# A transformer kernel in float32r: the two rings of split weight tiles are moved by 80 and by 208 bytes in SBUF

## The chip, the core and the metric

The kernel runs on one core of one Trainium2 chip. The metric is the device time of the program in microseconds. Three runs of the kernel before gave 2170.07, 2169.03 and 2170.19 us, median 2170.07 us.

## The reference

The input is a sequence of 256 tokens with 2048 features, batch 1. Everything is float32. The work is a chain of projections with small mixers between them:

```
h = rmsnorm(x);  proj = h @ w_in                      # 2048 x 7184
x = x + [stick_breaking(...), gated_delta(...)] @ w_out
x = x + cross_attention(rmsnorm(x), mem) @ w_xo
x = x + conv_ffn(rmsnorm(x)) : @ w_up (2048 x 11264), conv, silu, @ w_down
h = rmsnorm(x);  p = h @ fox_w_in                     # 2048 x 8224
x = x + (fox_attention(...) * silu(gate)) @ fox_w_out
h = rmsnorm(x);  p = h @ swa_w_in                     # 2048 x 4608
x = x + (window_attention(...) * silu(gate)) @ swa_w_out
return rmsnorm(x)
```

The weights come to about 370 MB and each is used once.

## The kernel before, in words

**The arithmetic.** Each float32 operand of a projection is split into two float32r tiles whose sum is close to it: hi (the value rounded to float32r) and lo (the rest). A product is taken as hi x hi + hi x lo + lo x hi, three passes in place of a slower full-float32 matmul.

**The weight stream.** SyncE loads the weights in order into `RAW`, a ring of `NRAW` = 5 tiles of 1024 floats in each of the 128 partitions. Each tile has two halves of 512 floats; there are 1416 halves in all (`HALVES`). For each half j ScalarE copies `RAW` to `WH[:, j % 6, :]` as float32r (the tile WH, line 1655, is the helper that records it), and VectorE subtracts `WL = RAW - WH` (line 987). The rings `WH` and `WL` hold `NW` = 6 halves each, 2048 bytes per partition and half. ScalarE works up to 5 halves ahead of TensorE (`HI_AHEAD`) and VectorE up to 4 (`LO_AHEAD`). SyncE refills a `RAW` tile when VectorE is done with it.

**The main matmuls.** `main(j)` of the TensorE program waits for `s_lo` to reach j + 1, that is for WL of half j, and then issues the matmuls of the half through the helper `mm` (line 510). A matmul has a stationary operand (loaded by LDWEIGHTS, 128 columns) and a moving operand. In the profile "main<-A,WH" means the output `main`, the moving tile A and the stationary tile WH. The activations lie in `A`, `B`, `H` and `M`; for each of their 128-row blocks 256 floats of hi and 256 floats of lo stand side by side, 2048 bytes in all. There are three forms of a half:

- wide (1184 halves, and 8 of the key and value projection of the window attention): 8 matmuls. WH is stationary and hi and lo of the activation move together (512 columns), twice; WL is stationary and hi moves (256 columns), twice; and all of this for two blocks, so 4 matmuls of 512 columns and 4 of 256.
- tokens (176 halves): 6 matmuls of 512 columns. The activation is stationary and WH, WL, WH move.
- plain or small (40 halves, and 8 more of the key and value projection, whose token part moves 256 columns): 12 matmuls of 256 columns.

That is 1192 x 8 + 176 x 6 + 48 x 12 = 9536 + 1056 + 576 = 11,168 main matmuls. The mixers and norms run between them in the same queues, in an order fixed when the program is built (`interleave`, with the tables `T_...`); their outputs are called `two`.

**Addresses.** The helper `at(name, kb, ...)` puts a tile at a base plus kb KB in every partition. All operands of main matmuls start at the base plus a multiple of 512 bytes: `A` at 16 KB, `B` and `H` at 48 KB, `M` at 80 KB, `RAW` at 163 KB, `WH` at 183 KB, `WL` at 195 KB, and within the tiles every slice starts at a multiple of 512 bytes. `WH` and `WL` are written by ScalarE and VectorE alone, and read by VectorE (WH) and TensorE (both). No DMA touches them.

Of the kernel before, what the change touches and what calls it, by code (L numbers as in the profile page):

```python
# [9 lines left out]
R = mybir.dt.float32r  # L10
# [5 lines left out]
NRAW, NW, HI_AHEAD, LO_AHEAD = 5, 6, 5, 4  # L16
# [249 lines left out]
def program(nc, xT, memT, ws, par, cst, g2, cscr, out):  # L266
    with ExitStack() as ctx:
# [44 lines left out]
        def at(name, kb, shape, dt=F):  # L312
            return nc.alloc_sbuf_tensor_at(name, [128] + shape, dt, offset=off0 + int(kb * 1024))
# [8 lines left out]
        RB, RB2 = at("RB", 160, [T]), at("RB2", 161, [T])  # L322
        SM = at("SM", 162, [256])
        RAW = at("RAW", 163, [NRAW, 1024])
        WH, WL = at("WH", 163 + 4 * NRAW, [NW, 512], R), at("WL", 163 + 4 * NRAW + 2 * NW, [NW, 512], R)

        M, MS = at("M", 80, [16, 2, T], R), at("MS", 112, [16, T])
        MH, ML = M[:, :, 0, :], M[:, :, 1, :]
# [1887 lines left out]
```

How the kernel before makes its waits and increments, by code:

```python
    def wait_ge(self, sem, value):  # L163
        if self.seen.get(sem.name, 0) < value:
            self.seen[sem.name] = value
            self.engine.wait_ge(sem, value)
# [288 lines left out]
        def sync_program(e):  # L455
# [2 lines left out]
            def load(i):  # L458
                if i >= NRAW:
                    w.wait_ge(s_lo, 2 * (i - NRAW) + 2)
                e.dma_start(RAW[:, i % NRAW, :], ws[i]).then_inc(s_raw[i % NRAW], 16)
# [15 lines left out]
            def swap(r):  # L477
                src, dst = wide_to(*ROPED[r]), ROT[r % 2]
                w.wait_ge(s_scl, SCALED[ROPED[r]])
                w.wait_ge(rp_zero, 1)
                if r >= 2:
                    w.wait_ge(rp_done, r - 1)
                for base in (0, 64):
                    lower, upper = slice(base, base + 8), slice(base + 8, base + 16)
                    e.dma_start(dst[lower, :, :], src[upper, :, :]).then_inc(s_rot[r % 2], 16)
                    e.dma_start(dst[upper, :, :], src[lower, :, :]).then_inc(s_rot[r % 2], 16)
# [6 lines left out]
                    e.dma_start(PAR[:, n:P_END], par[:, n:P_END]).then_inc(s_par2, 16)  # L494
                    e.dma_start(CST[:], cst).then_inc(s_cst, 16)
            for t, n, ve, ac in ((0, 0, 1, 0), (0, 3, 1, 1), (0, 1, 2, 1), (0, 2, 3, 1), (1, 0, 4, 1), (1, 1, 4, 2), (1, 3, 5, 2)):
                w.wait_ge(fin_ve, ve)
                w.wait_ge(fin_ac, ac)
                cols = slice(512 * n, 512 * n + 512)
                e.dma_start(out[128 * t:128 * t + 128, cols], YT[:, t, cols]).then_inc(s_out, 16)
            e.wait_ge(s_out, 128)
```

## Time and profile before

| | kernel before |
|---|---|
| device time, median of 3 | 2170.07 us |
| span of the profiled execution, first to last instruction | 2167.6 us |
| TensorE matmul (PE) busy | 2156.3 us, 99% |
| TensorE weight loads (PEld) busy | 1865.8 us, 86% |
| VectorE (DVE) busy | 1618.3 us, 75% |
| ScalarE (ACT) busy | 1327.2 us, 61% |
| GpSimd (POOL) busy | 9.7 us |
| moved by DMA | 389.31 MB, mean 180 GB/s |
| granted TensorE clock, mean | 0.999 |

How to read it: busy time counts from the start to the recorded end of each instruction. Matmuls overlap in the pipeline, so a matmul of 512 columns is recorded with some 395 ns although the next one starts after some 230 ns. What a stream of matmuls costs is therefore read from the distance between starts, not from the mean duration. The profile page gives no time of the profiled execution outside its span; the span lies 2.5 us below the median of the timed runs.

### The profile page before, as it was taken

How to read it: one execution, taken by the hardware profiler on the slowest of the kernel's cores; microseconds unless marked ns; L12 is line 12 of the kernel's file. 1: busy time of each engine (PE TensorE's matmuls, PEld its weight loads, DVE VectorE, ACT ScalarE, POOL GpSimd, SP SyncE). 2: the span in 40 equal slices, each digit the busy share in tenths (PEclk: the TensorE clock that was granted, in tenths of full speed). 3: DMA queues.
4: the chain of work that ended last, by engine and by line, in shares of the span. 5: the costliest groups of instructions: out<-in, count | busy, mean ns of one | idle time of the engine just before them, and what ended most of it. 6: DMA issues, size and time to landing. Idle time of an engine off the chain costs nothing.

```text
span 2167.6 us, 34503 instructions
## 1 busy us (share of the span) xinstructions
PE 2156.3 (99%) x13406; PEld 1865.8 (86%) x13406; DVE 1618.3 (75%) x2945; ACT 1327.2 (61%) x2601; POOL 9.7 (0%) x22
## 2 busy tenths in 40 slices
PE   9999999999999999999999999999999999999998
PEld 8888888888888888888888888888888888888887
DVE  7898666786688877655778867777676767688774
ACT  7866447775576666544666656555556655567764
POOL 0000000000000000000000000000000000000000
PEclk9999999999999999999999999999999999999999
DMA  7443434665455555555555555545554455544453
GB/s 279 169 146 137 147 115 141 218 217 186 156 190 189 188 191 186 193 185 192 187 191 189 185 194 185 193 171 197 181 177 174 167 192 186 189 161 155 146 200 140
DMA packets 107619, 389.31 MB, mean 180 GB/s; under 512 B 12304, under 2 KB 12560, under 8 KB 106688
## 3 DMA queue, kind: packets, MB, share of 16 engines
q1 hardware_dynamic: 105264, 377.31, 50.2%
q0 software_dynamic: 1904, 9.47, 1.2%
q8 instruction: 106, 1.74, 0.3%
q14 instruction: 57, 0.47, 0.1%
q10 hardware_dynamic: 288, 0.32, 0.0%
HBM read 384.34 MB, written 2.13 MB: 178 GB/s over the span
## 4 chain that ended last, share of the span: by engine, by line
PE 95%; DVE 3%; ACT 1%; issue 0%; DMA 0%; SPq 0%; DVEq 0%; ACTq 0%
PE main L510 88%; PE two L510 6%; PE two L513 1%; DVE WL L987 1%; DVE gt L987 0%; DMA RAW<-ws 0%; DVE GQ L993 0%; ACT L1654 0%; ACT WH L1655 0%; DVE GK L993 0%; PE main L556 0%; ACT PP L1655 0%; DVE PB L987 0%; ACT NT L1655 0%; DVE PP L993 0%
## 5 line engine op out<-in xcount | busy, mean ns | idle before, releaser
L1655 ACT ACTIVATE WH<-RAW 128x512 fp32r<-128x512 f32 x1416 | 882.1, 629 | 657.6 <-PE main L510 651.1
L987 DVE TENSOR_TENSOR WL<-RAW,WH 128x512 fp32r<-128x512 f32 x1416 | 961.2, 687 | 383.9 <-ACT WH L1655 374.4
L510 PE MATMUL main<-A,WH 128*128 128x512 f32 (+1 forms) x3680 | 1141.9, 393 | 1.0 <-DVE WL L987 1.0
L510 PEld LDWEIGHTS main<-A,WL 128*128 128x128 f32 x3584 | 673.9, 188 | 154.8
L510 PE MATMUL main<-A,WL 128*128 128x256 f32 x3584 | 713.7, 278 | 0.0
L510 PEld LDWEIGHTS main<-A,WH 128*128 128x128 f32 x3680 | 562.7, 189 | 13.8 <-issue 9.3
L510 PE MATMUL main<-H,WH 128*128 128x512 f32 x704 | 221.1, 395 | 0.0
L510 PE MATMUL main<-B,WH 128*128 128x512 f32 (+1 forms) x640 | 184.4, 373 | 0.0
L510 PEld LDWEIGHTS main<-H,WL 128*128 128x128 f32 x704 | 132.3, 188 | 31.3
L510 PE MATMUL main<-H,WL 128*128 128x256 f32 x704 | 138.4, 278 | 0.0
L510 PE MATMUL main<-WH,A 128*128 128x512 f32 (+1 forms) x448 | 137.6, 380 | 0.0
L510 PEld LDWEIGHTS main<-B,WL 128*128 128x128 f32 x576 | 108.5, 188 | 22.7
L510 PE MATMUL main<-B,WL 128*128 128x256 f32 x576 | 118.8, 279 | 0.0
L510 PEld LDWEIGHTS main<-H,WH 128*128 128x128 f32 x704 | 107.2, 189 | 0.0
L510 PEld LDWEIGHTS main<-B,WH 128*128 128x128 f32 x640 | 98.1, 189 | 0.2
L510 PEld LDWEIGHTS main<-WH,A 128*128 128x128 f32 x448 | 82.3, 188 | 15.4 <-DVE WL L987 0.5
L993 DVE SCALAR_TENSOR_TENSOR CC<-UB,PAR,CC 128x256 f32<-128x256 f32 x176 | 84.7, 481 | 3.1
L510 PE MATMUL main<-WL,A 128*128 128x512 f32 (+1 forms) x224 | 84.0, 375 | 0.0
L510 PE MATMUL main<-WH,B 128*128 128x512 f32 x256 | 80.2, 391 | 0.0
L510 PEld LDWEIGHTS main<-WH,B 128*128 128x128 f32 x256 | 48.1, 188 | 10.0 <-issue 0.2
L987 DVE TENSOR_TENSOR XT<-XT,main 128x512 f32<-128x512 f32 x72 | 49.1, 686 | 4.4 <-PE main L510 3.3
L1655 ACT ACTIVATE CC<-UB,PAR 128x256 f32<-128x256 f32 x88 | 51.7, 588 | 0.0
(322 smaller groups left out, 1722.5 us busy)
## 6 DMA issues: line engine op xcount, KB each, us to landing
RAW<-ws SPq DMA_DIRECT2D x707, 512.0 KB, 3.3
CB<-cscr POOLq DMA_DIRECT2D x4, 1024.0 KB, 4.7
XT<-xT POOLq DMA_DIRECT2D x4, 512.0 KB, 6.0
MS<-memT POOLq DMA_DIRECT2D x4, 512.0 KB, 8.7
xs<-xT SPq DMA_DIRECT2D x7, 256.0 KB, 7.6
out<-YT SPq DMA_DIRECT2D x7, 256.0 KB, 2.6
CST<-cst SPq DMA_DIRECT2D x1, 1248.0 KB, 7.9
G<-g POOLq DMA_DIRECT2D x1, 1024.0 KB, 5.9
```

What stands on the lines that cost most here:

```text
L510: return e.matmul(o, l, r, start=start, stop=True, skip_group_check=True)
L513: return e.transpose(o, i, ident)
L987: return e.tensor_tensor(o, a, b, op)
L993: return e.scalar_tensor_tensor(o, a, s, b, op0, op1)
L1655: return e.activation(o, i, f, bias=bias, scale=scale, accum_out=accum)
```

## The change

```
-        WH, WL = at("WH", 163 + 4 * NRAW, [NW, 512], R), at("WL", 163 + 4 * NRAW + 2 * NW, [NW, 512], R)
+        WHS, WLS = at("WH", 163 + 4 * NRAW, [512 * NW + 24], R), at("WL", 163 + 4 * NRAW + 2 * NW + 0.125, [512 * NW + 24], R)
+        WH, WL = (x[:, 20:20 + 512 * NW].rearrange("p (a b) -> p a b", b=512) for x in (WHS, WLS))
```

The two rings are allocated 24 floats (96 bytes) longer. The view of each begins 20 floats (80 bytes) into its allocation, and the allocation of WL begins 128 bytes later than before. So every half of WH lies 80 bytes further on than it did, and every half of WL 80 + 128 = 208 bytes further on. The halves are still 2048 bytes apart. `RAW` and the activations stay. No instruction is added, removed or moved on any engine, and no wait changes; only the start addresses of the operands WH and WL differ.

## Rows read from the trace of the kernel before

**Rows 1.** The page: span, busy time and the granted clock in 40 slices.
```profile
span 2167.6 us, 34503 instructions
PE 2156.3 (99%) x13406; PEld 1865.8 (86%) x13406; DVE 1618.3 (75%) x2945; ACT 1327.2 (61%) x2601; POOL 9.7 (0%) x22
...
PEclk9999999999999999999999999999999999999999
```

**Rows 2.** The page: chain of work that ended last, by engine and line.
```profile
PE 95%; DVE 3%; ACT 1%; issue 0%; DMA 0%; SPq 0%; DVEq 0%; ACTq 0%
```

**Rows 3.** Waits of PE: engine, line, waited for, total us, times, longest.
```profile
PE main L510 <- DVE WL L987: 1.0, 2, 0.5
```

**Rows 4.** Timeline of PE, a wide stretch: start, length, instruction, count.
```profile
1000.68 0.62 PE L510 MATMUL main<-H,WH 128*128 128x512 f32 x2
1001.14 0.40 PE L510 MATMUL main<-H,WL 128*128 128x256 f32 x2
1001.37 0.63 PE L510 MATMUL main<-H,WH 128*128 128x512 f32 x2
...
1004.16 0.63 PE L510 MATMUL main<-H,WH 128*128 128x512 f32 x2
```

**Rows 5.** Timeline of PE, a token stretch.
```profile
1406.66 0.39 PE L510 MATMUL main<-WL,A 128*128 128x512 f32 x1
1406.89 0.62 PE L510 MATMUL main<-WH,A 128*128 128x512 f32 x2
...
1411.42 0.39 PE L510 MATMUL main<-WL,A 128*128 128x512 f32 x1
```

**Rows 6.** Timeline of PE, two plain stretches.
```profile
25.45 0.40 PE L510 MATMUL main<-A,WH 128*128 128x256 f32 x2
25.69 0.28 PE L510 MATMUL main<-A,WL 128*128 128x256 f32 x1
...
28.33 0.40 PE L510 MATMUL main<-A,WH 128*128 128x256 f32 x2
...
581.86 0.40 PE L510 MATMUL main<-B,WH 128*128 128x256 f32 x2
...
583.66 0.40 PE L510 MATMUL main<-B,WH 128*128 128x256 f32 x2
```

**Rows 7.** Windows: stretch, us, busy per engine (count), clock, DMA share, GB/s.
```profile
26.00:28.00 2.00, 2.00 (x19) 2.00 (x19) 2.00 (x3) 1.87 (x4) 0.00 (x0) 1.00 0.98 404
582.00:584.00 2.00, 2.00 (x19) 2.00 (x18) 1.88 (x4) 1.00 (x2) 0.00 (x0) 1.00 0.00 0
```

**Rows 8.** Timeline of PE, float32 matmuls of the cross attention in a row.
```profile
577.82 3.18 PE L510 MATMUL two<-XPT,memV 128*128 128x256 f32 x14
```

**Rows 9.** The tile memV on PE: min/median/max ns, first and last start.
```profile
L510 PE MATMUL two<-XPT,memV x16: 377/379/380, 577.8 to 581.0; 128*128 128x256 f32 x16
```

**Rows 10.** Timeline of PE, float32r matmuls of the stick-breaking attention.
```profile
330.94 0.22 PE L510 MATMUL two<-SBH,NEGO 128*128 128x128 f32 x1
331.00 0.27 PE L510 MATMUL two<-SBL,NEGO 128*128 128x128 f32 x1
```

**Rows 11.** Timeline of PE, a token stretch just after an interruption.
```profile
1394.14 0.40 PE L510 MATMUL main<-WL,A 128*128 128x512 f32 x1
1394.37 0.62 PE L510 MATMUL main<-WH,A 128*128 128x512 f32 x2
...
1395.52 0.39 PE L510 MATMUL main<-WL,A 128*128 128x512 f32 x1
```

**Rows 12.** The page, part 5: busy us, mean ns of one, idle before, releaser.
```profile
L1655 ACT ACTIVATE WH<-RAW 128x512 fp32r<-128x512 f32 x1416 | 882.1, 629 | 657.6 <-PE main L510 651.1
L987 DVE TENSOR_TENSOR WL<-RAW,WH 128x512 fp32r<-128x512 f32 x1416 | 961.2, 687 | 383.9 <-ACT WH L1655 374.4
```

## The prediction

> **What bounds the kernel now.** I read the page's busy shares first. TensorE is busy for 2156.3 of 2167.6 us at the full granted clock in all 40 slices [rows 1]. The chain of waits then shows that 95% of what set the end is TensorE [rows 2]. The list of waits shows that TensorE waited for WL, the tile that each half needs last, for 1.0 us in the whole program [rows 3]. So the kernel lasts as long as the stream of matmuls lasts, and the question is what one main matmul costs from its start to the start of the next, because the change touches nothing but the addresses of one operand of each.
>
> The timelines give that distance. In the token form 21 matmuls lie between the starts at 1406.66 and 1411.42 us, so 4.76 / 21 = 226.7 ns for 512 columns [rows 5]. In the plain form 24 lie between 25.45 and 28.33, so 120.0 ns for 256 columns [rows 6]. The difference, 106.7 ns for 256 more columns, is 0.4167 ns a column, one column per cycle at the 2.4 GHz that the clock row grants. What is left is the same in both: 226.7 - 213.3 = 120.0 - 106.7 = 13.3 ns for each matmul that no column accounts for. In the wide form 20 matmuls lie between 1000.68 and 1004.16 [rows 4], five groups of two of 512 and two of 256 columns, 696 ns a group; longer stretches of the same pattern give 696.7. The columns take 640, so 56.7 / 4 = 14.2 ns are left for each matmul. Over the program that is 9536 x 14.2 + 1632 x 13.3 = 135.4 + 21.7 = 157 us, 7% of the span. This is the only thing that a shift of WH and WL could touch on the path.
>
> **The change part by part.** It adds no instruction, no wait and no DMA. Three kinds of access get a new start address.
>
> (a) ScalarE writes WH: 1416 times 629 ns. It idles 657.6 us before these, nearly all of it for TensorE to free a slot [rows 12]. (b) VectorE reads WH and writes WL: 1416 times 687 ns, with 383.9 us idle before them [rows 12]. I take both at zero. Their cover is that idle time, and the lead of 4 to 5 halves, about 1.39 us each, that the rings allow. Were (b) slower by a tenth, 1416 x 69 ns = 97 us more work would stand against those 383.9 us of idle time, and VectorE would be busy 79% instead of 75%. TensorE would see only what falls into the stretches where VectorE is full, such as 26 to 28 us [rows 7], at most a few us. A faster (a) or (b) is worth no more than the 1.0 us of rows 3. If TensorE gets faster, the cover shrinks: at 5% less time VectorE would be at 79% too, which still holds.
>
> (c) TensorE reads WH and WL, as stationary operand in the wide and plain forms and as moving operand in the token form. The trace of before has no main matmul whose operands start at anything but multiples of 512 bytes from one base, so the price of another start isn't in it, and I bound it from rows.
>
> What are the 13.3 to 14.2 ns? They are not other engines or DMA in the way. The plain form takes 120.0 ns between 26 and 28 us with DMA at 404 GB/s and ScalarE 94% busy, and again 1.80 us / 15 = 120.0 ns at 582 us with no DMA at all and ScalarE at half [rows 6, 7]. Nor are they what every weight change costs: the float32 matmuls on memV come 14 in 3.18 us, the last one counted with its whole 379 ns, so (3.18 - 0.38) / 13 = 215.4 ns each [rows 8, 9]. They have the same 128-column load and the same 512-byte starts, and if they stream their 256 columns twice (two records stand for each call), 213.3 ns are columns and 2.1 are left. And it isn't one constant: a float32r matmul of 128 columns was followed after 60 ns, 6.7 above its 53.3 [rows 10]. So the loss goes with float32r operands read at full rate while a load reads beside them. That can lie in the reading, which addresses might move, or in how the array takes in float32r weights, which they can't.
>
> *Fewer.* At the far end all but 2.1 ns goes: 9536 x 12.1 + 1632 x 11.2 = 133.7 us, giving 2036 us. With the 6.7 ns of rows 10: 9536 x 7.5 + 1632 x 6.6 = 82.3 us, giving 2088. With only the wide form brought down to the 13.3 of the other forms: 9536 x 0.9 = 8.6 us, giving 2161.5. *More.* Just after an interruption token matmuls came 6 in 1.38 us, 230 ns each, 3.3 above their steady 226.7 [rows 11]: the same operands, only the two streams of reads in another phase to each other. Paid always, that is 11,168 x 3.3 = 36.9 us, giving 2207.
>
> I take zero. The row nearest to "another relation of addresses" is the steady loss itself. It is 13.3 ns whether weights are stationary or moving, for slots of WH 2 KB apart and for slices that start 0, 512, 1024 and 1536 bytes into them. A read that depended on where its partner stands would be expected to show some spread over these, and 24 plain matmuls in a row show none. The sum is then 2167.6 + 0 for the span, which with the 2.5 us between span and median is 2170.1 us.
>
> The Trainium skill ("SBUF — State Buffer", section "Who interferes with whom") says that TensorE has two independent read ports, one for the moving operand and one for weight loads, and that it never waits on anyone. By that rule the change is worth nothing. The trace agrees that no other engine delays it, but it does show 13.3 ns a matmul that two independent ports would leave unexplained, where the same skill ("TensorE: Matmul & The Clock Gate", "Back-to-back issue gap") gives about 2.5 ns; so I don't let the rule decide.
>
> **The rivals.**
>
> *Faster: the loss is a collision of two reads at equal phase.* Both operands start at the same place within 512 bytes and both begin to be read at about the same moment, so load and stream may hit the same part of the memory again and again. With the weights 80 or 208 bytes further on they would pass each other. For it: the 2.1 ns left where the moving operand is read at half the rate, and the phase dependence in rows 11. Against it: the loss doesn't change with any step the trace holds, and two streams that stall each other once are out of phase from then on, whatever their addresses. Its price lies between the 8.6 us and the 82.3 us above; I name the middle, 45 us, 2125 us. That all of it goes (2036) is a small part of this case.
>
> *Slower: a read that begins off a boundary touches one piece more.* If TensorE fetches 64 bytes or more at once, a load of 512 bytes that starts 80 bytes in needs one more fetch, and so does each moving read of 1 or 2 KB in the token form. The place is each main matmul, where no slack covers it: the 0.2% that decides is 4.3 us / 11,168 = 0.39 ns, one cycle. With pieces of 128 bytes a load takes 5 instead of 4; if the loss goes with the pieces, a quarter of 13.3 is 3.3 ns, which is also the price of rows 11. The time lies between 2174 and 2207, and I name 2190. Against it: nothing in the trace speaks of such pieces.
>
> The Trainium skill ("SBUF — State Buffer", "The DMA port swizzle (why [64,N] ≈ [32,N])") gives the lines of SBUF 16 bytes. 80 and 208 are 5 and 13 of these, so by this rule no access touches a line more and this rival falls away. No row here shows the size of a line.
>
> *The change doesn't do what it says*, because the base is itself no multiple of 512: then only the distance between operands matters, and that does change, by 80 and 208. This gives no time of its own.
>
> **How the numbers follow.** A measurement of this kernel tells a change from none at about 0.2%, 4.3 us. No change, 2170: 0.45, with its own range of 2166 to 2174. Faster by the collision: 0.34, of which 0.07 lies below 2100. Slower by more pieces: 0.21, of which a good half lies below 2190. The effect has only to reach one cycle a matmul to leave the middle case, so I don't give that more. The range goes from 2100 to 2190 and leaves out 0.07 below and some 0.09 above.
>
> **What would show it.** If I am right, the starts in the same three stretches lie 226.7, 120.0 and 174.2 ns (the wide mean) apart again, and ScalarE and VectorE keep 629 and 687 ns. The collision is shown by shorter distances at the same clock, and best by a plain or token stretch below 13 ns of rest. The pieces are shown by longer ones in all forms. A change in 629 or 687 ns with TensorE unchanged would show that (a) or (b) is touched and covered. I am wrong if the distances move by as much as half a nanosecond, or if PE begins to wait for WL.

## The result and the profile after

The changed kernel takes 2179.38 us (median of 4, 2178.98 to 2179.54) where the kernel before takes 2169.8: a ratio of 1.0044, 95% interval 1.0032 to 1.0056. It is slower by 9.6 us. No change had been forecast, with 0.45; slower had 0.21.

The page of the changed kernel, its span, busy times and clock, answers to [rows 1]:

```profile
span 2177.7 us, 34503 instructions
...
PE 2165.4 (99%) x13406; PEld 1869.8 (86%) x13406; DVE 1619.7 (74%) x2945; ACT 1327.4 (61%) x2601; POOL 9.7 (0%) x22
...
PEclk9999999999999999999999999999999999999999
```

Its groups of the two ring operations answer to [rows 12]:

```profile
L1656 ACT ACTIVATE WH<-RAW 128x512 fp32r<-128x512 f32 x1416 | 882.5, 629 | 667.4 <-PE main L511 660.2
L988 DVE TENSOR_TENSOR WL<-RAW,WH 128x512 fp32r<-128x512 f32 x1416 | 962.2, 688 | 391.5 <-ACT WH L1656 381.1
```

ScalarE and VectorE take what they took, 629 and 688 ns; they only idle 10 and 8 us longer, which is the longer span. The clock is the same. What is new is the distance between the starts of matmuls. The timeline of PE in a wide stretch, against [rows 4]:

```profile
1005.29 0.62 PE L511 MATMUL main<-H,WH 128*128 128x512 f32 x2
1005.75 0.40 PE L511 MATMUL main<-H,WL 128*128 128x256 f32 x2
...
1009.49 0.62 PE L511 MATMUL main<-H,WH 128*128 128x512 f32 x2
```

Six groups of four in 4.20 us, 700.0 ns a group for 696.7, so 175.0 ns a matmul for 174.2. In a token stretch, against [rows 5]:

```profile
1416.71 0.40 PE L511 MATMUL main<-WL,A 128*128 128x512 f32 x1
...
1420.91 0.40 PE L511 MATMUL main<-WL,A 128*128 128x512 f32 x1
```

18 matmuls in 4.20 us, 233.3 ns for 226.7. Of the undisturbed token halves 73 take 1380 ns, which is 230.0 ns a matmul, and 27 take 1400, which is 233.3. And in two plain stretches, against [rows 6]:

```profile
25.24 0.40 PE L511 MATMUL main<-A,WH 128*128 128x256 f32 x2
...
28.42 0.40 PE L511 MATMUL main<-A,WH 128*128 128x256 f32 x2
...
586.07 0.40 PE L511 MATMUL main<-B,WH 128*128 128x256 f32 x2
...
589.67 0.40 PE L511 MATMUL main<-B,WH 128*128 128x256 f32 x2
```

27 matmuls in 3.18 us, 117.8 ns for 120.0, so faster; and 30 in 3.60 us, 120.0 as before. One change of address makes the wide and the token form dearer and one plain stretch cheaper.

Since both programs issue the same matmuls in the same order, the 13,405 distances can be subtracted one by one. The differences by form add up to the whole change of the span:

| distances | us |
|---|---|
| after wide matmuls | +6.78 |
| after token matmuls of 512 columns | +3.27 |
| after plain matmuls, and token ones of 256 columns | -1.04 |
| three long gaps at the program's start | +1.06 |
| everything else | +0.05 |
| sum | +10.12 (the spans: 2177.7 - 2167.6) |

The three gaps lie within the first 12 us. The waits for WL there rose from 1.0 to 2.1 us in all. In the other kernels below the same gaps grew by 0.05 to 1.7 us, by 0.5 us in the control e4, in which no steady distance changes, so they aren't put down to this change.

### The profile page after: what moved, and what is told of

Same layout as the page of the kernel before. It is cut to its first block, busy times and chain, and to the rows that moved or that the text cites. A ratio compares the mean times of both kernels' runs of the same rounds, so it can differ in the third digit from the quotient of the medians.

```text
span 2177.7 us, 34503 instructions
## 1 busy us (share of the span) xinstructions
PE 2165.4 (99%) x13406; PEld 1869.8 (86%) x13406; DVE 1619.7 (74%) x2945; ACT 1327.4 (61%) x2601; POOL 9.7 (0%) x22
## 4 chain that ended last, share of the span: by engine, by line
PE 95%; DVE 3%; ACT 1%; issue 0%; DMA 0%; SPq 0%; DVEq 0%; ACTq 0%
PE main L511 88%; PE two L511 6%; PE two L514 1%; DVE WL L988 1%; DVE gt L988 0%; DMA RAW<-ws 0%; DVE GQ L994 0%; ACT L1655 0%; ACT WH L1656 0%; DVE GK L994 0%; PE main L557 0%; ACT PP L1656 0%; DVE PB L988 0%; ACT NT L1656 0%; DVE PP L994 0%
```

## The experiments

Three theories went in. **D, distance**: the cost of a matmul depends on the distance between the start of the stationary and of the moving operand. **P, pieces**: each operand that starts off a boundary costs extra by itself. **N**: no address matters, only the history of the stream. Later ones are L and A (is it the weight load's reads, or the array) and M (several rhythms). The code is shortened: 183 and 195 stand for the sums of the kernel's line, and the `rearrange` of the change is left out.

### e1: a map of the shifts

```
for d in range(0, 128, 4): SECTIONS.append(("wide", d, 0, 48))     # stationary shifted by 4 d bytes
for d in range(0, 128, 4): SECTIONS.append(("plain", d, 0, 32))
for d in range(0, 128, 4): SECTIONS.append(("tokens", 0, d, 36))   # moving operand (the weights) shifted
...                                                                # wide, both or the moving operand shifted; shifts of 4 to 20 bytes
```

> A kernel of its own that computes nothing of the reference: streams of float32r matmuls on 128 rows and 128 stationary columns, in sections, with a pause between sections. Sections have the wide, plain and token forms of the kernel, with the stationary or the moving operand shifted by 0 to 496 bytes in steps of 16, a few with both shifted, and a few with shifts of 4 to 20 bytes. Theory D (distance): the two reads of TensorE meet in the memory, so the cost of a matmul varies up and down with the distance between the two starts, and both shifted by the same amount cost what no shift costs: wide 174.2 ns a matmul, plain 120.0, tokens 226.7 at distance 0, and some other distances cost less. Theory P (pieces): an operand that starts off a boundary costs more whatever the other does; then all shifts off the boundary cost the same, some 0.8 ns more in the wide form and 3 to 7 ns more in the token form, both shifted cost more still, and no shift costs less than 0. Theory N (no addresses): the times follow from the history of the stream alone; then every section of a form costs the same.

In the timeline of PE each section of one shape is one row: start, length, count. Two rows of the plain form (0 and 64 bytes), then four of the token form (0, 64, 240 and 256 bytes):

```profile
305.52 4.09 PE L82 MATMUL main<-A,W 128*128 128x256 f32 x32 [0.26 <-DVE T L69]
...
322.92 3.90 PE L82 MATMUL main<-A,W 128*128 128x256 f32 x32 [0.26 <-DVE T L69]
...
444.47 8.45 PE L82 MATMUL main<-W,A 128*128 128x512 f32 x36 [0.26 <-DVE T L69]
...
480.01 8.52 PE L82 MATMUL main<-W,A 128*128 128x512 f32 x36 [0.26 <-DVE T L69]
...
578.10 8.79 PE L82 MATMUL main<-W,A 128*128 128x512 f32 x36 [0.26 <-DVE T L69]
587.17 8.45 PE L82 MATMUL main<-W,A 128*128 128x512 f32 x36 [0.26 <-DVE T L69]
```

The lengths hold the first matmuls of each section too, so the steady distances of its last matmuls are used from here on, in ns:

| shift, bytes | 0 | 16 | 64 | 80 | 128 | 192 | 208 | 240 | 256 |
|---|---|---|---|---|---|---|---|---|---|
| wide, stationary shifted | 174.2 | 176.7 | 173.4 | 176.1 | 174.2 | 172.5 | 175.3 | 175.8 | 174.1 |
| plain, stationary shifted | 120.0 | 118.3 | 113.3 | 118.5 | 118.4 | 117.8 | 116.7 | 120.0 | 120.0 |
| tokens, moving shifted | 226.7 | 231.7 | 228.9 | 231.1 | 232.9 | 233.3 | 230.0 | 236.7 | 226.7 |

At shift 0 the bare streams give to a tenth what the kernel gives, so the loss belongs to TensorE alone. It goes up and down with the shift, and the token form repeats after 256 bytes at each of its 16 steps, to 0.1 ns. The two other forms repeat from 0 to 256 bytes, but not at each step: the wide form takes 176.7 ns at 160 bytes and 175.0 at 416, the plain form 113.3 at 64 and 117.8 at 320. Each section was started once here, and e12 shows that one start needn't speak for all. Both operands shifted alike by 32, 64, 128 or 256 bytes give 174.1 to 174.2, as none does; by 16 bytes 173.3 and by 80 bytes 175.0. N falls. P falls, since some shifts are cheaper. D holds in part: the relation of the two starts counts, but a common shift of 16 or 80 bytes isn't quite neutral, so the distance alone isn't all. That the two reads meet in the memory, as D has it, is not shown by this.

### e2, e3, e4: one ring at a time, and a control

```
e2:  WHS = at("WH", 183 + 64 / 1024, [512 * NW + 8], R);  WH = WHS[:, 4:4 + 512 * NW]     # 80 bytes;  WL: + 512 bytes
e3:  WH as before;  WLS = at("WL", 195 + 192 / 1024, [512 * NW + 8], R);  WL = WLS[:, 4:4 + 512 * NW]   # 208 bytes
e4:  WH and WL both + 512 bytes
```

> WH alone is shifted by 80 bytes; WL lies 512 bytes further on, which keeps it on a multiple of 512. Results of the changed kernel: wide halves 1400.0 ns for 1393.3, token halves 1380 to 1400 for 1360, plain halves on A 1413.6 for 1440. Theory D: half of the pairs of reads change their distance, WL keeps the old one; the wide half lands between or elsewhere (1385 to 1400), the time at 2165 to 2180 us. Theory P: half of the loads and all hi reads pay: wide 1396.7, about 2175 us. Theory N: 2169.8 or 2179.4 us, by the history only.

> WL alone is shifted by 208 bytes; WH stays. Theory D: again another mix of distances, 2165 to 2180 us, and with the kernel that shifts WH alone it need not add up to the 9.6 us of the change. Theory P: the other half of the loads pays, wide 1396.7 ns a half, about 2174 us, and the two single shifts add up to the 9.6 us. Theory N: 2169.8 or 2179.4 us.

> Both rings are shifted by 512 bytes, a control. Theory D and theory P, if the length that counts divides 512: nothing changes, halves at 1393.3, 1360 and 1440 ns, 2169.8 us within 0.1%. If a longer period than 512 bytes counts, or if any move of the rings changes the time, it differs by 0.2% or more.

| | us | ratio, 95% interval | wide half, ns | token half, ns |
|---|---|---|---|---|
| e2, WH + 80 | 2170.49 | 1.0003 (0.9993 to 1.0012) | 1387 to 1389, 1396 to 1397 | 1383 to 1391 |
| e3, WL + 208 | 2172.91 | 1.0014 (1.0005 to 1.0023) | 1393, some 1400 | 1387 |
| e4, both + 512 | 2169.85 | 0.9999 (0.9989 to 1.0008) | 1393 | 1360 |

The two single shifts cost 0.5 and 3.0 us against the same runs of the kernel before, together 3.5, where the change costs 9.6. The interval of e2 holds 1, so its time alone says little; its halves say more, since most are shorter than 1393 ns, where P had 1396.7. So the two don't add up, as P had them do, and what counts is a pattern over the reads of both rings. The control changes nothing: to move both rings by 512 bytes is free.

### e5: every pair of shifts

```
SECTIONS = [("wide", a, b, 40) for a in range(0, 256, 16) for b in range(0, 256, 16)]     # WH + a, WL + b
SECTIONS += [("tokens", a, b, 24) for a in range(0, 256, 16) for b in range(0, 256, 16)]
...
SECTIONS += [(f"w{w}", a, 0, 32) for w in (128, 256, 384, 512) for a in (0, 64, 80, 192)]     # w moving columns
```

> A kernel of its own that computes nothing of the reference: the streams of the first map again, now with two rings as in the kernel, every pair of shifts of WH and WL from 0 to 240 bytes in steps of 16, in the wide and the token form, and four widths of the moving operand. Theory D (distance, read by read): each load meets the moving read that runs beside it, so the cost of a wide group depends on both shifts and is not the sum of the two single ones; the pair (80, 208) shows the 175.0 ns a matmul that the changed kernel shows, (80, 0) and (0, 208) show less, as the two kernels with one ring shifted do. Equal shifts repeat the first map: 64 gives 173.4 and 192 gives 172.5 ns. Theory P (pieces) has fallen already if shifts of 64 and 192 are again below 174.2. The part above the columns should be about 7 ns for 128 moving columns and 13 from 256 on, if it belongs to the load that runs beside, and grow with the width if it belongs to the moving read alone.

| WH, WL | 0, 0 | 80, 208 | 80, 0 | 0, 208 | 64, 64 | 192, 192 | 128, 240 | 240, 192 | 64, 0 |
|---|---|---|---|---|---|---|---|---|---|
| wide, ns | 174.1 | 175.0 | 173.8 | 174.2 | 173.4 | 172.5 | 171.6 | 171.7 | 178.3 |
| tokens, ns | 226.7 | 230.0 | 230.9 | 230.9 | 228.8 | 233.3 | 231.2 | 233.3 | 233.3 |

The pair of the change shows its 175.0. Priced with 9536 wide and 1056 token matmuls, some 205 of the 256 pairs would be slower than no shift by more than 4.3 us, some 40 within that and some ten faster. In the token form no pair is below the 226.7 of equal starts. For an arbitrary shift, slower was the likely result. Each pair was started once, and the two that the map made the fastest, (128, 240) and (240, 192), are slower than no shift in the kernel (e9, e10).

The widths went against what [rows 10] had suggested. A stream of 128 moving columns comes every 111.7 ns, 58 above its columns, at all four shifts tried; 256 columns lose 6.7 to 13.3 and 512 columns 13.4 to 20.0 with the shift. The single 60 ns of [rows 10] was one distance between others, and no steady cost.

### e6 and e7: equal shifts of 64 and of 192 bytes

```
WHS = at("WH", 183 + 192 / 1024, [512 * NW], R);  WLS = at("WL", 195 + 192 / 1024, [512 * NW], R)     # e7; e6 with 64
```

> Both rings shifted by 64 bytes. Theory D with the numbers of the first map: wide 173.4 for 174.2 ns, 9536 x 0.8 = 7.6 us less; tokens 228.9 for 226.7, 1056 x 2.2 = 2.3 us more; plain up to 6.7 less on 576, at most 3.8 us less. Sum: 5.3 to 9.1 us faster, 2161 to 2165 us. Theory P: slower, 2174 us or more. Theory N: as before.

> Both rings shifted by 192 bytes. Theory D with the numbers of the first map: wide 172.5 for 174.2 ns, 9536 x 1.7 = 16.2 us less; tokens 233.3 for 226.7, 1056 x 6.7 = 7.0 us more; plain 2.3 less on 576, 1.3 us less. Sum: 10.5 us faster, 2159.5 us. Theory P: slower, 2174 us or more. Theory N: as before.

e6 takes 2162.72 us, ratio 0.9966 (0.9954 to 0.9979); e7 takes 2160.94 us, ratio 0.9958 (0.9945 to 0.9972). Both were forecast from the map, 2161 to 2165 and 2159.5. Both are faster than both kernels of this case. The timeline of e7 in a wide stretch:

```profile
899.94 0.62 PE L513 MATMUL main<-H,WH 128*128 128x512 f32 x2
...
903.39 0.62 PE L513 MATMUL main<-H,WH 128*128 128x512 f32 x2
```

20 matmuls in 3.45 us, 172.5 ns; its token halves take 1400 ns for 1360.

### e8: which operand, which type

```
SECTIONS = [("r", w, c, s, 32) for w in (512, 256) for c in (32, 64, 96, 128) for s in (0, 64, 80, 128, 192, 240)]   # float32r, c stationary columns
SECTIONS += [("f", w, 128, s, 24) ...]   # float32
SECTIONS += [("b", w, 128, s, 32) ...]   # bfloat16
SECTIONS += [("r", 512, 128, s, 32) for s in range(0, 64, 4)]
```

> A kernel of its own that computes nothing of the reference: streams of matmuls with 512 and 256 moving columns, with 32, 64, 96 and 128 stationary columns and six shifts of the stationary operand, in float32r; the same with 128 stationary columns in float32 and bfloat16; and shifts of 0 to 60 bytes in steps of 4. Theory L (the reads of the load that runs beside hold up the moving read): the part above the columns falls with the number of stationary columns, 13.4 ns with 128, some 6.7 with 64 and 3.4 with 32 at shift 0, and depends on the shift; bfloat16, whose operands are half as many bytes, loses less than half and float32 next to nothing. Theory A (the array takes in float32r weights slowly): the part is the same 13.4 ns with 32 as with 128 stationary columns, or follows the columns without any dependence on the shift.

The timeline of PE, whole sections: float32r with 32 stationary columns (shifts 64 and 80), with 128 (0 and 64), float32 with 256 columns (0 and 64), and bfloat16 (128 and 240; in the first of these two one record is missing):

```profile
33.07 7.60 PE L70 MATMUL main<-A,WH 128*32 128x512 f32 x32 [0.26 <-DVE T L59]
40.96 7.52 PE L70 MATMUL main<-A,WH 128*32 128x512 f32 x32 [0.26 <-DVE T L59]
...
167.26 7.57 PE L70 MATMUL main<-A,WH 128*128 128x512 f32 x32 [0.26 <-DVE T L59]
175.12 7.74 PE L70 MATMUL main<-A,WH 128*128 128x512 f32 x32 [0.26 <-DVE T L59]
...
443.82 10.63 PE L70 MATMUL main<-AF,WF 128*128 128x256 f32 x48 [0.26 <-DVE T L59]
454.73 10.63 PE L70 MATMUL main<-AF,WF 128*128 128x256 f32 x48 [0.26 <-DVE T L59]
...
566.92 7.08 PE L70 MATMUL main<-AB,WB 128*128 128x512 bf16 x31 [0.26 <-DVE T L59]
...
581.66 7.08 PE L70 MATMUL main<-AB,WB 128*128 128x512 bf16 x32 [0.26 <-DVE T L59]
```

Steady distances above the columns, for 512 moving columns in float32r: 13.3 to 20.0 with 128 stationary columns, 13.3 to 20.0 with 96, 15.0 to 22.2 with 64 and 15.6 to 18.3 with 32. A quarter of the load costs no less here. With 256 moving columns a smaller load costs somewhat less: the mean loss over the six shifts is 11.6 ns with 128 stationary columns, 10.6 with 96, 9.6 with 64 and 8.1 with 32, where L had a quarter. So L falls in its main point: the loss isn't in proportion to what the load reads, though at 256 columns it falls with it. A falls as well: the loss depends on the shift at every number of columns. bfloat16 takes 215.8 ns at all six shifts, 2.5 above its columns, and float32 takes 215.8 for 256 columns and 429.2 for 512, at all six shifts too. With 256 and 512 columns and over these six shifts, float32r is the only one of the three types that has the loss and feels the address. Even 4 bytes count: float32r with 512 columns takes 226.7 at 0 and 232.3 at 4 bytes.

### e9, e10, e11: the best and the worst pairs of the map in the kernel

```
e9:   WH + 128, WL + 240      e10:  WH + 240, WL + 448      e11:  WH + 64, WL + 512     (bytes)
```

> WH shifted by 128 bytes and WL by 240, the best pair of the map of pairs. Theory L with the map: wide 171.6 for 174.1 ns a matmul, 9536 x 2.5 = 23.8 us less; tokens 231.2 for 226.7, 1056 x 4.5 = 4.7 us more; sum 19 us faster, 2151 us. If the map's single value was a chance of how the section began, the time is anywhere from 2155 to 2175 us.

> WH shifted by 240 bytes and WL by 448, which is 192 in a period of 256: the second best pair of the map. Wide 171.7 for 174.1 ns, 22.9 us less; tokens 233.3, 7.0 us more; sum 16 us faster, 2154 us.

> WH shifted by 64 bytes, WL by 512, so by 0 in the period: the worst pair of the map. Wide 178.3 for 174.1 ns, 40 us more; tokens 233.3, 7 us more; sum 47 us slower, 2217 us. Theory P, which counts each start by itself, would put it between the kernel before and the one with both rings shifted by 64, 2163 to 2170 us.

e11 came nearly as priced: 2210.45 us for 2217, ratio 1.0183 (1.0169 to 1.0197), wide halves 1427 ns. But e9 takes 2176.7 us, ratio 1.0028 (1.0018 to 1.0039), and e10 2176.84, ratio 1.0031 (1.002 to 1.0043): slower by some 6 us where 19 and 16 less were expected, and e9 also lies outside the 2155 to 2175 us that its expectation kept for the case of chance. The timeline of e9 shows why, in two wide stretches:

```profile
899.63 0.63 PE L513 MATMUL main<-H,WH 128*128 128x512 f32 x2
...
903.14 0.64 PE L513 MATMUL main<-H,WH 128*128 128x512 f32 x2
...
1760.20 0.61 PE L513 MATMUL main<-B,WH 128*128 128x512 f32 x2
...
1763.63 0.61 PE L513 MATMUL main<-B,WH 128*128 128x512 f32 x2
```

3.51 us for 20 matmuls, 175.5 to rounding (halves of 1407 ns, 175.9), and 3.43 us, 171.5 (halves of 1373). The relative addresses are the same in both. Of its undisturbed wide halves 725 take 1406 or 1407 ns and 267 take 1373 or 1374. The stretches are long: 526 halves in a row from 626 us on take 1406 or 1407, 92 in a row from 1723 us on 1373 or 1374. No two halves that follow each other undisturbed lie on different levels; between a stretch of one and a stretch of the other there is always an interruption by a mixer. e10 has both levels too, 1400 ns in 785 halves and 1373 or 1374 in 133.

### e12: the same pairs, started at different moments

```
+ e.matmul(main[:, 1, 0:first], WH[:, 0:128], A[:, 0:first], ...)      # first = 32, 56, ... 296 columns, ahead of each section
PAIRS = [(0, 0), (80, 208), (80, 0), (192, 192), (128, 240), (240, 192), (64, 0)]
```

> A kernel of its own that computes nothing of the reference: the wide form with seven pairs of shifts, each started twelve times behind one float32r matmul of another width (32 to 296 columns), 56 matmuls each; and the token form with three pairs. Theory M (several steady rhythms): the addresses decide which rhythms exist, the moment at which a stream starts decides which of them it falls into. Then the pair (128, 240) shows 171.6 ns a matmul in some of its twelve sections and 175.9 in others, as the kernel with this pair did in its stretches (halves of 1373 and 1407 ns), (240, 192) shows 171.6 and 175.0, and the pair (0, 0) and (192, 192), whose kernels showed one level each (1393 and 1380 ns), keep to 174.2 and 172.5 nearly always. The pair (80, 208) of the change shows 175.0. Theory D alone (addresses decide everything): one level for each pair, the same in all twelve sections, and what the kernels showed of two levels came from their other instructions.

The timeline of PE in two sections with the pair (128, 240), the first started behind 32 columns, the second behind 152:

```profile
522.96 0.63 PE L76 MATMUL main<-A,WH 128*128 128x512 f32 x2
...
528.59 0.63 PE L76 MATMUL main<-A,WH 128*128 128x512 f32 x2
...
575.29 0.61 PE L76 MATMUL main<-A,WH 128*128 128x512 f32 x2
...
580.78 0.61 PE L76 MATMUL main<-A,WH 128*128 128x512 f32 x2
```

32 matmuls in 5.63 us, 175.9 ns, and in 5.49 us, 171.6. Steady distances over the twelve starts:

| wide, WH, WL | ns, in how many of twelve sections |
|---|---|
| 0, 0 | 174.2 in 12 |
| 80, 208 | 175.0 in 12 |
| 80, 0 | 173.9 in 12 |
| 192, 192 | 172.5 in 12 |
| 128, 240 | 175.8 in 7, 171.7 in 5 |
| 240, 192 | 175.0 in 7, 171.7 in 5 |
| 64, 0 | 178.3 in 12 |

The token form has 226.7 in 12 with (0, 0), 233.3 in 12 with (192, 192), and 230.0 in 10 and 233.3 in 2 with (80, 208); the changed kernel has both of these, in halves of 1380 and 1400 ns. M holds for the pairs tried: the addresses decide which steady rhythms exist, and the start of a stream decides which of them it falls into. It kept to it for as long as it ran undisturbed, here and in e9.

## Why the prediction was wrong

**What bounds the kernel.** Right. Of the 10.1 us of the span 9.0 are distance between the matmuls of running streams and 1.1 are the gaps at the start. One cycle a matmul was rightly named as enough to decide: the 9.0 us over 11,168 main matmuls are 0.8 ns, two cycles.

**(a) and (b), ScalarE and VectorE.** Right: 629 and 688 ns, the added work is none, and the waits for WL rose by 1.1 us, at the program's start, as they do in other kernels.

**(c), the loss of 13.3 to 14.2 ns.** The first two readings held. It has nothing to do with other engines or DMA: the bare streams of e1 repeat it to 0.1 ns. And it goes with float32r: e8 gives 2.5 ns for bfloat16 and for each record of float32 with 256 or 512 columns at the same starts, where the prediction had read 2.1 for float32. The Trainium skill ("TensorE: Matmul & The Clock Gate", section "Back-to-back issue gap") gives this 2.5 ns over the columns for an isolated matmul, and some 131 ns a matmul for a stream of loads and matmuls with 512 columns. The streams of e8, a load for each matmul, take 215.8 ns in bfloat16, as by the first figure and not by the second, and 226.7 in float32r, as by neither. The third reading, of [rows 10], was wrong: a single distance was taken for a steady cost, and a stream of 128 columns takes 111.7 ns (e5).

**The value zero.** This is the step that failed: "The row nearest to 'another relation of addresses' is the steady loss itself", and that the loss was the same for slots 2 KB apart and for slices 0, 512, 1024 and 1536 bytes in. All these steps are multiples of 512 bytes. By e4 a move of 512 bytes costs nothing, and by e1 256 bytes from equal starts cost nothing either, so the rows showed one phase of the pattern only. They could not speak for shifts of 80 or 208, and the same argument had also been turned against the collision rival. With no row at another phase there was no ground for the middle case over the outer ones. What the runs showed in its place: at shifts of 80 and 208 bytes a wide matmul takes 175.0 ns for 174.2 and a token matmul 230.0 or 233.3 for 226.7, which makes most of the 9.6 us.

**The collision rival.** Its first half was near the truth: the cost does depend on the distance between the starts. Its sign was wrong. Equal starts are no bad case but a good one, the best of all in the token form, and only some shifts beat it in the wide form. The objection that two streams that stall each other once are out of phase from then on "whatever their addresses" was wrong too: they settle into a rhythm, and which ones there are depends on the addresses (e12). That a collision of two reads is what makes the loss stays unshown.

**The pieces rival.** It forecast slower, from 2174 us on, and the time is slower by 9.6; the upper part of the stated range, in which the 2179.4 us lie, came from it alone. That is luck, since its mechanism isn't there. With pieces of 128 bytes, e6 and e7 start off the same boundaries and are faster. With pieces of 64 bytes, 208 bytes lie off a boundary and 192 don't, and the token form takes 230.0 ns at 208 and 233.3 at 192 (e1). And e2 and e3 don't add up to the change. The upper bound from [rows 11], 3.3 ns a matmul, sized a loss that came out at 0.8 ns in the wide form and 3.3 to 6.7 in the token form. The Trainium skill ("SBUF — State Buffer", section "The DMA port swizzle (why [64,N] ≈ [32,N])") speaks of lines of 16 bytes. By them a shift of 80 bytes touches no more lines and this rival falls, and fall it does. But lines alone don't describe the rest: shifts by whole lines take the token form from 226.7 to 236.7 ns (e1), and 4 bytes, off the start of a line, cost 5.6 ns with 512 columns (e8) and save 0.9 in the wide form (e1, 173.3 for 174.2).

**What is open.** Which part of TensorE's float32r path keeps these rhythms isn't known, nor whether the two reads hold each other up. Each matmul had its own weight load, and a stream without loads wasn't tried. Only the pairs of e12 were started more than once. One hint lies in the first microseconds of the programs, where TensorE ran at half its later rate. The kernel before, main matmuls of 256 columns:

```profile
6.69 0.41 PE L510 MATMUL main<-A,WL 128*128 128x256 f32 x1
6.90 0.59 PE L510 MATMUL main<-A,WH 128*128 128x256 f32 x2
7.33 0.28 PE L510 MATMUL main<-A,WL 128*128 128x256 f32 x1
```

Three in 0.64 us are 213 ns each, twice the 106.7 of the columns and nothing above. The first wide section of e1 shows the same, 12 matmuls in 3.84 us from 17.32 us on, 320.0 ns each, which is twice the 160.0 of the columns, where 174.2 follow later. So at equal starts the loss is no fixed time or number of cycles for each float32r matmul: it came only at the full rate. The profile's rows give a granted clock of 1.00 for both stretches all the same, so the rate is read from the distances alone. It wasn't tried to steer a stream of the pair (128, 240) into its better rhythm inside the kernel.

## What to carry to other kernels

Before reading "the cost doesn't depend on the address" from a trace, ask at which steps the addresses in it differ; here every step was a multiple of 512 bytes, and the trace was silent. When TensorE is the bound and streams float32r, the offset between the two operands is worth a map in bare matmuls, with each shift started at several moments: a shift with one rhythm in all starts transferred to the kernel here, as 192, 192 and 64, 0 did, while 128, 240 and 240, 192, with two, came out otherwise than priced. Equal starts were a good default here.

## What the runs showed of the hardware

- float32r matmuls with 128 rows and 128 stationary columns, 256 or 512 moving columns, one load each, lose 13.3 ns at equal starts and 6.7 to 23.3 ns at other offsets (113.3 ns for 256 columns at 64 bytes, 236.7 for 512 at 240, e1), against 2.5 ns in bfloat16 (e8). Many of the steady values are multiples of 6.67 ns, 16 cycles at 2.4 GHz: 6.7, 13.3 and 20.0.
- In the first microseconds, with matmuls at half the rate, float32r matmuls with equal starts lost nothing: 213 ns for 256 columns (kernel before) and 320.0 ns for the wide mean (e1).
- The token form repeats with a shift of 256 bytes (e1), and 512 bytes are free (e4).
- A stream of 128 moving columns came every 111.7 ns in float32r and in float32, and the moving columns were 53.3 of these. 256 float32r columns came every 113.3 ns at a shift of 64 bytes: twice the columns for 1.6 ns more (e5, e8).
- A program of fixed instructions and addresses can run at two speeds in different stretches, 1373 and 1407 ns a half in e9, kept for up to 92 and 526 halves on end.
